# Two heads at a time in attention, rotation by DMA, and a resequenced first projection, in a three-block transformer kernel

## The reference

```python
def nsa_mixer(h, cos, sin, w_in, cmp_pe, cmp_w1, cmp_w2, gate_b, w_o):
    q, kc, vc, ks, vs, kw, vw, gt = jnp.split(h @ w_in, splits, axis=-1)
    # q, kc, ks, kw are rotated: x1*c - x2*s, x2*c + x1*s
    def compress(t, pe, w1, w2):       # blocks of 32 tokens, stride 16: 15 blocks
        blk = (t[:, :, cidx] + pe).reshape(b, g, n_cmp, CMP_LEN * hd)
        return jax.nn.gelu(blk @ w1) @ w2
    kc = compress(kc, cmp_pe[0], cmp_w1[0], cmp_w2[0])
    vc = compress(vc, cmp_pe[1], cmp_w1[1], cmp_w2[1])
    p_cmp = masked_softmax(s_cmp, cmask)
    o_cmp = ...                        # over the 15 blocks
    o_slc = ...                        # 256 tokens are 4 blocks of 64, all are selected: causal
    o_win = banded_attention(q, kw, vw, WIN_LEN)     # window 512 > 256: causal
    o = gates[..., 0, None] * o_cmp + gates[..., 1, None] * o_slc + gates[..., 2, None] * o_win
    return from_q_groups(o) @ w_o

def swa_mixer(h, cos, sin, w_qkv, b_qkv, sinks, w_o, b_o):
    q, k, v = jnp.split(h @ w_qkv + b_qkv, ..., axis=-1)
    o = banded_attention(rope(q), rope(k), v, SWA_WINDOW, sinks.reshape(g, r))  # window 128
    return from_q_groups(o) @ w_o + b_o
```

## Time and profile before

| what | value |
|---|---|
| time, median of 3 runs | 1273.41 us (1273.21 to 1273.92) |
| the profiled execution: its own time, its span | 1273.24 us, 1271.4 us |
| busy, share of span | PE 94%, PE weight loads 89%, DVE 60%, ACT 44%, POOL 36% |
| the chain that ended last | PE 81%, DVE 8%, ACT 3%, issue 3%, POOL 3%, DMA 1% |

### The profile page before, as it was taken

One profiled execution on the slowest core, in us unless ns is written; L12 is line 12 of the kernel. 1 busy time (PEld: TensorE's weight loads), 2 busy tenths in 40 slices (PEclk: granted clock), 3 DMA queues, 4 the chain that ended last, 5 costly groups with the idle time before them and its releaser, 6 DMA issues.

```text
span 1271.4 us, 23862 instructions
## 1 busy us (share of the span) xinstructions
PE 1195.2 (94%) x9313; PEld 1130.8 (89%) x9313; DVE 765.0 (60%) x1093; ACT 565.6 (44%) x788; POOL 452.6 (36%) x430
## 2 busy tenths in 40 slices
PE   6998999999999888999999999998988898999996
PEld 5987678999999875999999998988978896999996
DVE  5753564767655566676765464436755657777544
ACT  4232344554544444455454336644353444545432
POOL 4522232266630433166651211113431303666401
PEclk9998799999999989999999999998999999999998
DMA  6651001666645540466665453243341453667551
GB/s 200 205 192 41 9 26 34 200 176 188 188 160 183 164 134 2 120 178 187 177 197 182 149 173 127 69 129 104 101 133 34 148 165 87 191 174 196 180 169 50
DMA packets 224581, 175.49 MB, mean 138 GB/s; under 512 B 7796, under 2 KB 205788, under 8 KB 224380
## 3 DMA queue, kind: packets, MB, share of 16 engines
q1 hardware_dynamic: 219052, 168.33, 44.4%
q10 hardware_dynamic: 5424, 6.09, 1.4%
q0 software_dynamic: 32, 0.03, 0.0%
HBM read 173.39 MB, written 1.05 MB: 137 GB/s over the span
## 4 chain that ended last, share of the span: by engine, by line
PE 81%; DVE 8%; ACT 3%; issue 3%; POOL 3%; DMA 1%; SPq 0%; ACTq 0%; DVEq 0%; POOLq 0%
PE bank L574 22%; PE bank L580 22%; PE bank L575 21%; PE bank L840 2%; DVE w_l L1512 2%; ACT w_h L1157 2%; PE bank L608 2%; PE bank L614 1%; PE bank L704 1%; PE bank L1013 1%; PE bank L808 1%; POOL work L2261 1%; DVE work L1627 1%; PE bank L848 1%; PE bank L692 1%
## 5 line engine op out<-in xcount | busy, mean ns | idle before, releaser
L574 PE MATMUL bank<-xh,w_h 128*128 128x256 f32 (+2 forms) x1792 | 451.6, 289 | 5.5 <-DVE xl L1530 4.1
L575 PE MATMUL bank<-xl,w_h 128*128 128x256 f32 (+2 forms) x1792 | 443.0, 284 | 0.0
L574 PEld LDWEIGHTS bank<-xh,w_h 128*128 128x128 f32 x1792 | 339.9, 190 | 8.5 <-issue 5.1
L575 PEld LDWEIGHTS bank<-xl,w_h 128*128 128x128 f32 x1792 | 340.8, 190 | 1.0
L1512 DVE TENSOR_TENSOR w_l<-raw,w_h 128x2048 fp32r<-128x2048 f32 (+3 forms) x95 | 212.2, 2234 | 158.6 <-ACT w_h L1157 158.5
L1157 ACT ACTIVATE w_h<-raw 128x2048 fp32r<-128x2048 f32 (+3 forms) x95 | 173.3, 1825 | 241.7 <-PE bank L580 220.5
L580 PE MATMUL bank<-xh,w_l 128*128 128x256 f32 (+2 forms) x1792 | 251.4, 283 | 2.9 <-DVE w_l L1512 2.9
L580 PEld LDWEIGHTS bank<-xh,w_l 128*128 128x128 f32 x1792 | 230.5, 189 | 3.3 <-DVE w_l L1512 3.1
L2183 POOL TENSOR_TENSOR work<-work 128x256 f32<-128x256 f32 x66 | 162.9, 2469 | 140.4 <-ACT work L1300 140.4
L1795 DVE TENSOR_TENSOR w_l<-raw,w_h 128x2048 fp32r<-128x2048 f32 x66 | 151.4, 2293 | 14.0 <-ACT w_h L1296 13.8
L574 PE MATMUL bank<-hid_h,w_h 128*128 128x256 f32 (+1 forms) x592 | 148.0, 284 | 2.5 <-issue 1.8
(11 more groups left out here) (291 smaller groups left out, 1595.9 us busy)
## 6 DMA issues: line engine op xcount, KB each, us to landing
raw<-in_ffn_w_gu SPq DMA_DIRECT2D x88, 512.0 KB, 5.0
raw<-in_w_in SPq DMA_DIRECT2D x26, 1024.0 KB, 5.2
raw<-in_ffn_w_down SPq DMA_DIRECT2D x40, 512.0 KB, 4.6
raw<-in_w_ffn_up SPq DMA_DIRECT2D x22, 512.0 KB, 4.1
raw<-in_w_ffn_gate SPq DMA_DIRECT2D x22, 512.0 KB, 5.3
raw<-in_nsa_w_in SPq DMA_DIRECT2D x10, 1024.0 KB, 5.4
raw<-in_w_ffn_down SPq DMA_DIRECT2D x20, 512.0 KB, 4.4
raw<-in_swa_w_qkv SPq DMA_DIRECT2D x5, 1024.0 KB, 5.3
```

The source lines that it names most:

```text
L574: mm(dst, parts[0][:, k, cols], high, start=first, stop=False)
L575: mm(dst, parts[0][:, k, cols], low, start=False, stop=False)
```

## The change

- Heads in pairs: keys are stored once, head a's in rows 64a to 64a+63. Score matmuls use 64 rows, alternate between the two heads and write two banks; value matmuls alternate between heads too (`value_piece`). S_p and S_pt get four buffers. In NSA one of three transposed parts is copied by ScalarE. SWA takes a whole chunk (both heads, all queries) as one pair, `pair_scores` to `pair_values`; GpSimd scales it in four pieces; scores of pairs 0 and 1 are issued among the projections.
- First layer resequenced: keys and values to be compressed, then queries, gates, the other keys, the other values. All of the compressed branch stands among the chunks.
- `compress`: the blocks are stationary (61 columns, the 61st is the position offset, which becomes gelu's bias), the weights move with 256 columns; keys write partitions 0 to 60 and values 64 to 124 of one bank. The block copies are now 32 plain copies on ScalarE.
- Rotation: four SBUF to SBUF DMAs of 32 rows by 256, issued by ScalarE (`rotate`), into `xr`; the sign is in the sine table. `permute` goes.
- Output projection's slabs 11 and 12 are converted in quarters in the NSA loop (`high_piece`, `low_piece`).
- `keep_busy` matmuls are 384 columns, not 512; the two calls in the third block go from 8 to 11 and from 14 to 19, the first layer's goes.

```diff
-        for c0 in range(1024, 2560, 256):
+        for c0 in (1024, 1280, 0, 256, 512, 768):
             plain(w_in, c0, c0 + 256)
         plain(w_in, 2560, 2608)
-        for i in range(4):
-            plain(w_in, 256 * i, 256 * i + 256)
+        for c0 in (1536, 2048, 1792, 2304):
+            plain(w_in, c0, c0 + 256)
...
-        NSA = [(8, 1), (9, 1), (10, 0), (11, 0), ("k", 0), ("k", 2), (12, 0), (13, 0), ("k", 4), ("k", 6), (14, 0), (15, 0),
-               (16, 0)] + [(i, 1) for i in range(8)]
+        NSA = [(8, 1), (9, 1), (10, 0), (11, 0)] + [(i, 1) for i in range(8)] + [(16, 0), ("k", 0), ("k", 2), ("k", 4), ("k", 6),
+               (12, 0), (13, 0), (14, 0), (15, 0)]
...
-            def permute(after):
-
-                k = rope["k"]
-                pe.wait_ge(*after)
-                if k >= 2:
-                    pe.wait_ge(sin_done, k - 1)
-                mm(bank[4 + k % 2][:, 0:T1], E("rot"), xs[:, k % 2, :], start=True, stop=True).then_inc(perm_done, 1)
-                rope["k"] += 1
...
+            def compress(half):
+
+                pe.wait_ge(blk_ready, 16)
+                for kv in range(2):
+                    pe.wait_ge(cmp_loaded[kv], 16 * (half + 1))
                 for p in range(8 * half, 8 * half + 8):
-                    for hc in range(2):
-
-                        last = mm(bank[7 - kv][:, 60 * hc:60 * hc + 60], w1[:, p % 8, 128 * hc:128 * hc + 128],
-                                  blkT[:, kv, p, :], start=p == 0 and hc == 0, stop=p == 15, skip_group_check=True)
+                    for kv in range(2):
+                        last = mm(bank[7][64 * kv:64 * kv + 61, 0:256], blkT[:, kv, p, :], cmp_w[:, kv, p % 8, :],
+                                  start=p == 0, stop=p == 15, skip_group_check=True)
                 last.then_inc(cmp_hid, 1)
...
+            def value_piece(O, a, qb, pt, w, kb, g, first=False):
+
+                return mm(O[64 * a:64 * a + 64, 128 * qb:128 * qb + 128], vtok[:, w, kb, 64 * g:64 * g + 64], pt,
+                          start=first, stop=True, skip_group_check=True)
...
+            def first_scores(ci):
+
+                if ci:
+                    pe.wait_ge(at_exp, 3 * ci - 2)
+                pe.wait_ge(roped, 13 if ci < 4 else 14)
+                for a in range(2):
+                    mm(bank[4 + a][:, 0:256], ident_b[:, :], each(causal, 2), start=True, stop=False, skip_group_check=True)
+                for b in range(2):
+                    for a in range(2):
+                        last = mm(bank[4 + a][:, 128 * b:128 * b + 128], q_half(ci, a, 0), k_half(4 * b + ci // 2, a, 128),
+                                  start=False, stop=True, skip_group_check=True)
+                last.then_inc(at_scores, 1)
+
+            def second_scores(ci):
+
+                if ci:
+                    pe.wait_ge(at_exp, 3 * ci)
+                else:
+                    pe.wait_ge(cmp_pt, 2)
+                for a in range(2):
+                    mm(bank[6 + a][:, :].rearrange("p (b k) -> p b k", b=2)[:, :, 128:256], ident_b[:, :], each(causal, 2),
+                       start=True, stop=False, skip_group_check=True)
+                for b in range(2):
+                    for a in range(2):
+                        ins = mm(bank[6 + a][:, 256 * b:256 * b + 256], q_half(ci, a, 1), k_half(4 * b + ci // 2, a, 256),
+                                 start=False, stop=True, skip_group_check=True)
+                        if b:
+                            ins.then_inc(at_scores, 1)
...
+            pe.wait_ge(vt_taken, 3)
+            for i in range(1, 8 + 2):
+                if i <= 8:
+                    part_turn(3 * i - 3)
+                if i < 8:
+                    first_scores(i)
+                if i >= 2:
+                    second_values(i - 2)
+                if i <= 8:
+                    part_turn(3 * i - 2)
+                if i < 8:
+                    second_scores(i)
+                if i <= 8:
+                    first_values(i - 1)
+                    part_turn(3 * i - 1)
...
+            def swa_attention():
+
+                for i in range(2, 8 + 2):
+                    pair_turn(i - 2)
+                    if i < 8:
+                        pair_scores(i)
+                    pair_values(i - 2)
...
+                if n == 6:
+                    pair_scores(0)
+                if n == 8:
+                    pe.wait_ge(vt_taken, 4)
+                    pair_scores(1)
...
+            def rotate(ready):
+
+                k = rope["k"]
+                act.wait_ge(*ready)
+                if k >= 2:
+                    act.wait_ge(sin_done, k - 1)
+                for b in range(4):
+                    act.dma_start(xr[32 * b:32 * b + 32, k % 2, :], xs[32 * (b ^ 1):32 * (b ^ 1) + 32, k % 4, :])\
+                        .then_inc(turned_round[k % 2], 16)
+                rope["k"] += 1
...
+            for kv in range(2):
+                load_cmp(kv, 0)
+            rotate((proj_taken, 1))
+            rotate((proj_taken, 2))
+            high(2)
+            high(3)
+            act.wait_ge(meta_ss, 1)
+            line.put(fn(meta_rstd[:, :], bank[6][:, 0:META], ACT.Sqrt, bias=eps_col[:, 0:1]), meta_root)
+            act.wait_ge(proj_taken, 4)
+            blocks(1)
+            act.wait_ge(roped, 2)
+            blocks(0)
+            rotate((proj_taken, 5))
+            high(4)
+            rotate((proj_taken, 6))
+            rotate((proj_taken, 7))
+            high(5)
+            rotate((proj_taken, 8))
+            rotate((proj_taken, 9))
+            high(6)
...
-                t = xs[:, (NSA_ROPED + rope) % 2, :] if r else big1[:, place, :]
+                t = xs[:, rope["k"] % 4, :] if r else big1[:, place, :]
                 line.put(fn(t, t, ACT.Identity, bias=vec("bqkv", 8 if n == 0 else 9 if n == 1 else n - 2)), biased)
-                rope += r
+                if r:
+                    rotate((biased, n + 1))
                 if n % 2:
                     high(M_SWA + 2 + n // 2)
                 if n == 3:
                     act.wait_ge(vt_done, 4)
...
-                dve.wait_ge(perm_done, k + 1)
+                dve.wait_ge(turned_round[k % 2], 64 * (k // 2 + 1))
                 if k >= 2:
                     dve.wait_ge(roped, k - 1)
-                line.put(V.tensor_tensor(tsin[:, k % 2, :], bank[4 + k % 2][:, 0:T1], E("sin"), ALU.mult), sin_done)
+                line.put(V.tensor_tensor(tsin[:, k % 2, :], xr[:, k % 2, :], E("sin"), ALU.mult), sin_done)
                 rope["k"] += 1
...
+                if i == 16:
+                    cmp_softmax()
+                if i == 17:
+                    cmp_norm()
+                if i == 19:
+                    part_max(0)
+                if i == 20:
+                    part_factor(0)
...
+            def pair_factor(v):
+
+                dve.wait_ge(at_exp, V_SWA + v + 1)
+                dve.wait_ge(at_sinkexp, v + 1)
+                den, r = st_den[:, v % 4, :], st_r[:, v % 4, :]
+                if v >= 4:
+                    dve.wait_ge(at_probs, V_SWA + 2 * (v - 4) + 2)
+                line.put(V.tensor_tensor(den, den, st_es[:, v % 4, :], ALU.add))
+                line.settle()
+                line.put(V.reciprocal(r, den), at_r)
...
+            def swa_extra(i):
+                if i % 2:
+                    low(M_SWA + 2 + i // 2)
+                if i == 1:
+                    dve.wait_ge(small_loaded, 16 * SMALL_DMAS)
+                    line.put(V.tensor_scalar(nsinks, sinks, -1.0, None, ALU.mult))
+                if i == 7:
+                    pair_max(0)
+                if i == 9:
+                    pair_factor(0)
+                    pair_max(1)
 
...
```

724 lines of the change are left out of this document (380 added, 344 removed).

## The result

The changed kernel took 1285.61 us (median of 8 runs, 1271.48 to 1286.77), the kernel before 1273.3 (8 runs, 1272.31 to 1273.92). The ratio is 1.0066 with an interval of 1.0038 to 1.0095: slower by 0.7%, where 1.3% faster was forecast. The profiled execution happens to be the shortest of the eight, 1271.48 us. So there are two questions: why its span of 1269.7 us isn't near 1255, and why most executions are longer still. For the second I profiled the unchanged file twice more; these two profiles stand here as the repeats.

The account below looks back on a forecast made before the run. TensorE (busy 94% of the span) was taken to bound the kernel, with VectorE and ScalarE binding the new loops. 1273.2 less 24.4 (first layer) plus 8.5 (second layer) gave 1257 us, range 1232 to 1276.

Parts of the forecast that it names:

- First layer, 24.4 forecast: First layer's projections and attention: out-projection to start at 181.7 instead of 206.1, 24.4 us less.
- Part 2: Everything from the second layer's out-projection on; only filler matmuls were said to change there, 0.1 us.
- The waits: TensorE's waits in the first layer's projections, on rotation, block copies, compress loads, gates and compressed probabilities: 19.4 us.
- the pair: One head pair of the first attention, bound by a ring of VectorE and ScalarE: 6.9 us, against 9.02 before.
- A: Mark in the profile: start of the first layer's out-projection, forecast at 181.7 us, 206.1 before.
- Second layer, 8.5 forecast: Second layer's projections and attention: first turn 12 us later, end at 512.7 plus 1.5 for the clock, 8.5 us more.
- The chain: Second-layer projections: take, biases, two rotations of 1.6 us on ScalarE, high and low, 8.8 us for two chunks.
- The loop behind: Second attention after its first turn: a ring of 3.95 us a pair, then 5.9 of run-out, ending at 512.7.
- B: Rival: issuing costs ScalarE nearly nothing, so the second layer takes 13.4 us less; 1234 us, chance 0.22.
- D: Rival: the clock stays at its lower level in the attention loop, eight pairs add 33 us; 1290 us, chance 0.12.
- C: Rival: no change, the start costs more through slower block copies or loads at half rate; 1272 us, chance 0.11.
- The size taken for the row halves: First attention's score matmuls on two row halves run side by side, worth half their streaming, 1.3 us a pair.

Follow-up runs that it names:

- run 3: Changed kernel with each rotation of both layers as one DMA of 128 partitions, not four of 32, rows copied unrotated (results wrong): median 1262.75 us.
- Runs 9: Changed kernel with every rotation a TensorE matmul: 1257.04 us; also with earlier compress loads and softmax and a later last conversion: 1239.84 us.
- run 10: Filler matmuls added: 84 in the changed kernel's wait before second-layer probabilities, 1280.01 us; 24 in the kernel before, ahead of the second out-projection, 1277.90 us.
- run 6: Changed kernel with second-layer rotations issued by SyncE and VectorE making the low part before it waits for the rotation: median 1261.82 us, ratio 0.9898.
- run 2: Changed kernel with the second layer's nine rotations issued by SyncE instead of ScalarE: median 1274.47 us.
- run 4: Changed kernel with a pair's score matmuls head after head instead of alternating between the two heads: median 1283.90 us.

## Why the prediction was wrong

Forecast were 1257 us, the median is 1285.6. The profiled execution, 1271.5, is 8.4 us over the forecast in the first layer, 8.1 over it in the second and 2.3 under it in Part 2; the other 14.1 us lie between it and the median.

**First layer, 24.4 forecast, 16.05 measured.** The forecast had chunk 20 end at 126.6; it ends at 130.7. The waits were 3.3, 0.5, 9.4, 1.8, 0.3 and 8.3, together 23.6 against 19.4. The queue's order was right: the rotation behind two compress loads landed just before 37.8, 36.8 forecast. That the first wait came out at 3.3 against 3.2 is luck all the same, since it was ended by ScalarE's conversion, late behind 6.03 us of issuing; in run 3, where issuing is short, the wait is 3.3 us too, and there it is the low part behind the landing that ends it. The second loads were issued at 67.0, not 64, since ScalarE was held by rotations, and ScalarE, behind two more rotations, reached the conversion of slab 10, on which VectorE's softmax stood waiting, at 110.3 only. TensorE worked some 18 us at the lower clock after these waits (37 to 43, 77 to 81, 91 to 94, 120 to 125), which costs 9 us where 5 were taken. The work itself was 4 us less than summed. From there to the out-projection 59.4 us against 55.1: the pair was 7.08 against 6.9 (eight times 0.2), the rest is the start of the loop, where the first pair's turns wait 1.9 us on the value copies on ScalarE and the clock falls once more (granted 0.55 to 0.60 over 135 to 139). The price of an issue isn't all of the miss here: in run 3 a rotation holds ScalarE for less than the forecast's 1.6 us, and A is 184.6, still 2.9 behind the 181.7 forecast.

**Second layer, 8.5 forecast, 16.6 measured.** The step that failed is "One issue there takes 0.49; I take 0.40 (bounds 0 if issuing hides, 0.49)". It took 0.61, above the upper bound: of a rotation's four issues the first takes 0.51 and the three behind it 0.61 each, and the 0.49 was read from one row. The chain was rightly drawn: with 0.61 it is 8.8 + 4 x 2 x 0.21 = 10.5 us for two chunks, measured 10.7. Four such rounds and the last rotation add 4 x 1.9 + 0.8 = 8.4 us; the first turn came 19.9 us later where 12 were forecast, 7.9 more. (The 8.5 itself is a slip: 512.7 + 1.5 - 505.9 = 8.3.) The loop behind was near the forecast, 30.4 us from turn to out-projection (29.2), against 33.7 before.

**Rivals.** B fell: issuing is not free, the next ScalarE row waits for it ("<-issue", 2.5 us). D fell as stated: the loop from 141 to 190 kept the full clock in all three profiles (to 188 in the second repeat). C was the nearest in time for the profiled execution, and by another mechanism: the start was 4.1 us later than forecast, but it was the second layer that gave everything back. For the median D was nearest in time, and its mechanism did not happen. The size taken for the row halves (1.3 us, 1.27 measured) and the pair (6.9, 7.08 measured) held.

**Part 2, taken as unchanged.** This is the second step that failed, "Part 2 of the kernel changes only the filler matmuls", at 0.1 us. In the profiled run it was 2.2 us shorter than before, in the repeats 5.9 and 8.0 us longer. In the profiles this, with the low stretch at the first out-projection, makes up nearly all between 1271 and the 1281 and 1289 of the repeats; for the other runs near 1285 it is inferred. The range of 1232 to 1276 had no term for it: it took the clock's low stretches outside the changed stages as fixed, and the three runs of before, within 0.7 us, suggested so.

**What stays open.** What brings the low stretch near 951 to 972, and whether the change makes it more frequent: both repeats have it and the first profile hasn't, the one profile of the kernel before hasn't, and of that kernel's other runs only the times are known, most of them near 1273 and some up to 1282. Runs 9 and 10 show that the idle TensorE isn't needed, and run 10 that the change isn't needed; that the moment at which Part 2 starts decides is compatible with it, but a start at 489.4 (run 3, with the stretch) and one at 489.6 (run 6, without) speak against the moment alone. That is not settled.

## What to carry to other kernels

Price a DMA that stands in an engine's own program by its issues, from rows where as many stand one behind another, and count them in the chain of that engine; a rotation's four issues between two activations (2.44 us) cost more than the conversion they stood beside (1.91). When work leaves a busy engine, see what is queued behind it where it lands: the second layer's rotations cost 18 us more on ScalarE than on TensorE, which they had left, 10 more on SyncE, and nothing more on SyncE once VectorE made the next low part ahead of the product that waits for them. In the first layer, with nearly the same orders, A was 183.4 with the rotations on SyncE and 173.5 with them on TensorE. And profile a kernel more than once before explaining a difference of under 1%: here unchanged code moved by 10 us between profiles.

## What the runs showed of the hardware

- A DMA issue for 32 partitions of 1 KB took ScalarE 0.51 us as the first of four and 0.61 behind another; one for 128 partitions took 0.47 alone and 0.61 behind another (run 3). Single issues took longer in the first layer, 1.53 and 1.90 us right behind the two pairs of 1 MB compress loads, 1.36 and 1.40 elsewhere; why is not shown. The Trainium skill (DMA: Bandwidth & Descriptors, Issuing engines are not separate DMA queues) calls the time to initiate a DMA usually small relative to the DMA itself. For a single issue this case agrees: 0.61 us of issuing, 2.5 us (median) from issue to landing. For the four of a rotation taken together it doesn't: in run 2 the first four took 2.5 us, from 428.66 to 431.1, and the product that waits for them began 2.4 us later, at 433.57; there the measurement decides.
- Score passes of 64 rows started in pairs, 7 to 14 ns apart, with some 112 ns from pair to pair of 128-column passes, where passes of 128 rows came 112 ns apart singly: two in the time of one, in whichever order they stood within their group (run 4).
- The granted clock fell for 21 us in Part 2 while TensorE was busy throughout (21.00 of 21 us), in code made of many small matmuls, in some executions and not in others. Part 2 took 763.4 to 765.7 us in the profiles without that stretch and 771.6 or more in those with it.
